# Layer 1's attention: the projection piece that fills in stands ahead of the preceding unit's outputs instead of behind them

## The reference, cut to what matters

```
# 256 positions, 12 self heads and 4 memory heads of 64 numbers; w_in is 1024 x (3*768 + 256)
h = x @ b_w_in
q, k, v, q_mem = split(h, [768, 1536, 2304])
mix     = moba_attention(q, k, v)              # 256 positions are one block: plain causal softmax attention
mem_out = memory_cross_attention(q_mem, mem, w_mem_kv)   # softmax over 256 memory rows, 4 heads
sub = concat([mix, mem_out]) @ w_mix_out
x = layer_norm(ALPHA * x + sub, ...)
x = layer_norm(ALPHA * x + swiglu(x, ...), ...)
```

## Time and profile before

| what | value |
|---|---|
| median of 3 runs | 1921.5 us (1921.12 to 1921.51) |
| span of the profiled execution | 1919.6 us, 1.9 us below the median of the runs |
| PE busy over the span | 1826.0 us, 95% |
| DVE, ACT busy | 785.6 us, 570.1 us |
| layer 1's attention, from `pT0` to `pr0` | 1629.8 to 1705.0 us: 75.2 us, PE busy 68.2 us |
| from there to the end | 1705.0 to 1919.0 us: 214.0 us, PE busy 205.3 us |

### The profile page before, as it was taken

One profiled execution on the slowest core, in us unless ns is written; L12 is line 12 of the kernel. 1 busy time (PEld: TensorE's weight loads), 2 busy tenths in 40 slices (PEclk: granted clock), 3 DMA queues, 4 the chain that ended last, 5 costly groups with the idle time before them and its releaser, 6 DMA issues. The chain is left out here.

```text
span 1919.6 us, 24342 instructions
## 1 busy us (share of the span) xinstructions
PE 1826.0 (95%) x9814; PEld 1167.5 (61%) x9814; DVE 785.6 (41%) x1150; ACT 570.1 (30%) x911; POOL 17.0 (1%) x33
## 2 busy tenths in 40 slices
PE   7999999999999999999999999999999999999998
PEld 6799888743333333333333333337888888878886
DVE  6867655411111111111111111115676656666665
ACT  4444554310101000001010010004555544545552
POOL 1000001000000000000000000000000000000000
PEclk7999999999999999999999999999999999999999
DMA  9976756599999999999999999997456646336552
GB/s 343 323 251 230 243 176 217 208 429 428 431 431 430 430 430 431 429 432 431 429 431 431 431 430 430 430 420 233 132 176 197 187 165 219 111 110 198 184 178 99
DMA packets 155400, 592.36 MB, mean 309 GB/s; under 512 B 6703, under 2 KB 85743, under 8 KB 128832
## 3 DMA queue, kind: packets, MB, share of 16 engines
q1 hardware_dynamic: 152816, 582.90, 77.3%
q0 software_dynamic: 2512, 8.45, 1.4%
HBM read 590.26 MB, written 1.07 MB: 308 GB/s over the span
## 5 line engine op out<-in xcount | busy, mean ns | idle before, releaser
L1674 PE MATMUL psum<-shared,expert_arena 128*64 128x512 f32 x1536 | 341.5, 596 | 23.0 <-DMA shared<-in_w_mlp_dram 23.0
L1533 DVE TENSOR_SCALAR expert_arena<-psum 128x512 f32<-128x512 f32 x32 | 22.1, 692 | 583.7 <-PE psum L1674 583.7
L1674 PEld LDWEIGHTS psum<-shared,expert_arena 128*64 128x64 f32 x1536 | 105.5, 137 | 242.5 <-issue 198.8
L415 PE MATMUL psum<-layer_x_parts,layer_w_hi 128*128 128x512 f32 x704 | 240.5, 396 | 0.4 <-DVE layer_x_parts L2144 0.4
L1439 ACT ACTIVATE expert_arena<-expert_arena 128x512 f32<-128x512 f32 x32 | 20.1, 629 | 562.5 <-DVE expert_arena L1533 562.5
L414 PE MATMUL psum<-layer_x_parts,layer_w_lo 128*128 128x256 f32 x616 | 171.8, 279 | 0.0
L352 DVE TENSOR_TENSOR mixer_w_lo<-mixer_ring,mixer_w_hi 128x1024 fp32r<-128x1024 f32 x96 | 116.4, 1223 | 96.7 <-ACT mixer_w_hi L347 96.4
L352 DVE TENSOR_TENSOR layer_w_lo<-slots_ahead,layer_w_hi 128x1024 fp32r<-128x1024 f32 x96 | 116.9, 1224 | 94.5 <-ACT layer_w_hi L347 94.5
L347 ACT CAST mixer_w_hi<-mixer_ring 128x1024 fp32r<-128x1024 f32 x96 | 100.0, 1048 | 158.1 <-PE psum L385 94.2
L415 PEld LDWEIGHTS psum<-layer_x_parts,layer_w_hi 128*128 128x128 f32 x704 | 125.8, 188 | 24.6 <-DVE layer_x_parts L2144 0.8
L383 PE MATMUL psum<-layer_w_hi,layer_x_parts 128*128 128x512 f32 (+1 forms) x384 | 138.7, 361 | 0.4 <-DVE layer_x_parts L2144 0.4
(11 more groups left out here) (311 smaller groups left out, 2683.0 us busy)
## 6 DMA issues: line engine op xcount, KB each, us to landing
shared<-in_w_mlp_dram SPq DMA_DIRECT2D x98, 2048.0 KB, 22.0
expert_ring<-in_w_mlp_dram SPq DMA_DIRECT2D x64, 2048.0 KB, 25.4
mixer_ring<-in_w_in_dram SPq DMA_DIRECT2D x38, 1024.0 KB, 6.3
slots_ahead<-in_w_mlp_dram SPq DMA_DIRECT2D x15, 2048.0 KB, 25.7
mixer_ring<-in_w_ada_dram SPq DMA_DIRECT2D x22, 1024.0 KB, 6.2
slots_ahead<-in_w_ffn_in_dram SPq DMA_DIRECT2D x21, 1024.0 KB, 4.9
memory_kv<-in_w_mlp_dram SPq DMA_DIRECT2D x15, 1024.0 KB, 24.7
kept<-in_w_mlp_dram SPq DMA_DIRECT2D x15, 1024.0 KB, 26.7
```

The lines of the kernel that those rows point to most:

```text
L415: last = self.nc.tensor.matmul(out, hi, both[:, k].rearrange("p h s -> p (h s)"), start=k == 0, stop=k == KC - 1)
L1533: nc.vector.tensor_scalar(glu, both[:, :, 0], LIMIT, None, ALU.min).then_inc(glu_ready, 1)
L1674: last = nc.tensor.matmul(U[CAP * h:CAP * h + CAP, N * n:N * n + N], xg[:, k, j, :], expert_slot(M, k // 2)[:, at:at + N], start=False, st ...
```

## The change

One line moves. In the loop over the units, the call that appends the next piece of the projection, `some()`, now comes ahead of the job `ao{u-1}`, not behind it.

```
@@ -1872,9 +1872,9 @@
                 weights_over(u - 1)
             if u < len(units):
                 scores(u)
+            some()
             if u:
                 jobs.add(f"ao{u - 1}", "dve", high=True)
-            some()
             if u == len(units) - 3:
                 some()
         assert not fill
```

## The result

The changed kernel takes 1938.0 us, the median of 5 runs (1937.4 to 1942.8), against 1921.5 us (5 runs). The ratio is 1.0086, with an interval of 1.0075 to 1.0097: slower by 16.5 us. Forecast were +9.0 us and a range up to 1936.0, so the time lies outside it.

What follows compares the result with a forecast made beforehand. PE was taken to bound the stage and the one behind. New waits of 15.07 us less 5.19 and 0.89 saved, with no clock fall, gave +9.0 us: 1930.5 us from 1921.5, range 1928.0 to 1936.0.

Steps and rivals of the forecast that it cites:

- PE sets the pace in this stage and behind it: Layer 1's attention and the stage behind: PE, not transfers, is the bound, so added PE waiting moves the end equally.
- The chain behind the outputs: Transposes pT1, pT2, pT3, pT4, pT6 wait for divide, now behind splits and outputs' subtraction: five new waits, 15.07 us.
- What goes: PE's old waits for copies at ao0, ao1, ao2, ao4, ao6 and unit 4's scores: 5.19 us saved, plus 0.89.
- The sum of +9.0: Whole stage: 15.07 us of new waits less 5.19 and 0.89 saved, good to about 1.5 us either way.
- The clock: PE's granted clock in the new waits: no fall taken, 0 us; at most five falls of 5.1 us, 25 us.
- Rival B: The clock falls to 1.2 GHz in the longest wait or two: 1935.6 us, or 1932 to 1935 if partly; chance 0.19.
- C: Outputs not held by the splits, so the chain begins when outputs end, transposes at E + 3.43: 1925.7 us; chance 0.07.
- D: divide(u) done in time, transposes don't wait and only 6.1 us of old waits go: 1915.4 us; chance 0.04.

Runs made afterwards that it cites:

- early divide: The changed kernel with layer 1's divide(u) on DVE directly behind the mask and maximum of sb{u}; 1916.7 us against 1922.5 for the kernel before.
- divide ahead of the subtraction: The changed kernel with divide(u) ahead of the subtraction of ao{u-1}, behind both weight splits, and 5, 4, 6, 4, 4 dummies in the five waits; 1929.9 us.
- waits filled: The changed kernel with 6, 5, 7, 5 and 5 dummy matmuls in PE's five new waits; 1933.0 us against 1922.5 for the kernel before.

## Why the prediction was wrong, point by point

- **PE sets the pace in this stage and behind it.** Right. The stage is 16.1 us longer and the median 16.5, and what lies behind the stage takes 214.7 us in both.
- **The chain behind the outputs.** Right in place and in size: five waits, released by L2106, 14.9 us against 15.07, in the order of sizes that was said. Shown by the early divide, which takes them all away, and by divide ahead of the subtraction, which takes 1.7 us off.
- **What goes.** Right in place: all the waits named are gone. In size it is too large: with the early divide, where these go and no new wait comes, the stage is 4.7 us shorter, not the 6.1 of the sum. The pieces of the next point are 0.5 of that.
- **The sum of +9.0.** Small by 1.0 (10.0 by the parts, +9.8 with the waits filled). A piece that is followed by outputs instead of transposes holds PE 5.94 us, not the 5.86 that I read from a piece followed by transposes, six times 0.08. In the second chain the last cast comes 0.44 us behind the outputs' start and not 0.16 as in the others, which makes 0.27. The handover from DVE to PE is 0.15, not the 0.06 of the earlier trace rows, which cancels against the earlier start of the cast (E + 0.16, not E + 0.25). The last 0.2 to 0.3 us are not traced. All of it is inside the 1.5 us that the prediction allowed.
- **The clock: the step that failed.** "I take none, by the nearest row: 2.36 us did not bring a fall." The term of the clock was put at nothing, and in the changed kernel it is 6.1 us: four falls of 1.5 to 1.6 us. One wait that brought no fall is no bound, since the same wait brings a fall in one execution and none in another. The very wait of the earlier trace rows did so in eight of fourteen profiles. Within the stage the runs show falls behind 1.74, 2.61, 2.89, 3.15, 3.63 and 3.64 us and none behind three waits of 3.14, one of 2.89, one of 2.61 and four of 1.46 to 1.62 us. Five such waits brought four falls in each of two profiles. The Trainium skill's rule that I weighed and set aside ("TensorE: Matmul & The Clock Gate", section "HAM oscillation — how this bites in real kernels") was the better guide for what would happen. By it the long waits could each bring a fall, anew each time. The traces agree in part: 3.15, 3.63 and 3.64 us did so, 3.14 us did not, three times. That waits of 1.7 to 2.9 us bring falls as well is measured here alone.
- **Rival B**, at 0.19, had the mechanism, with both sizes off. It spoke of the longest wait or two, and there were four falls. It priced one at up to 5.1 us, as if a whole piece ran at 1.2 GHz, and it is 1.5 us, since the clock is back before the piece ends. That its 1935.6 comes near the 1938.0 is luck: the two errors nearly cancel. With four falls at their measured 6.1 us in all, the forecast would have been 1936.6, still 0.6 outside the range; the chain's 1.0 us and the 0.4 between stage and medians are the rest. The number of falls was the term to carry with both its ends, none and five.
- **Rivals C and D** were rightly held low. C's waits near 2 us did not come. D's time, 1915.4, nearly came out, not in this kernel but in the one that meets its condition: divide behind the exponentials and ahead of the outputs, 1916.7.

## What to carry to other kernels

When filler work is moved to cover one wait, look at what it covered where it stood: the trace shows no wait there, and the cover is the distance between when the input is ready (1657.87) and when the engine comes for it (1658.24). Then read who else is written ahead of the released instruction on its own engine; here a division that had its inputs for over 5 us (at u = 3 of the changed kernel the last exponential ends at 1665.4 and the multiplication starts at 1670.96) stood behind work on the outputs and the weights, and moving it turned a change that loses 16.5 us into one that gains 5.8. Price a new wait of PE of 2 us or more not at its length alone but as a range: its length without a fall of the clock, and its length plus the price of one, 1.5 us here. One row with a long wait and no fall does not close that range.

## What the runs showed of the hardware

- The granted clock fell behind waits of PE as short as 1.74 us in dense work. Behind the waits of this stage it fell between 0.4 us before and 1.6 us after PE's new start, so that it cost work and hardly any idle time: 1.5 to 1.6 us each, in a fall of 3.4 us.
- Whether it falls behind a given wait differs between executions of one program: behind 3.15 us in one, not behind 3.14 us in the other. One wait of 1.85 to 2.44 us, in code that all kernels share, brought a fall in eight of fourteen profiles. What in a run decides it stays open.
- Dummy matmuls in a wait keep the clock up for the price of sizing them. With nearly full waits there was no fall (three profiles of five waits each), with waits left at 1.5 to 1.7 us one in five, and with 12 us too many the kernel was slower by that.
